# TensorE's usual expert path placed directly behind its test, and the keys of the last attention projected once and copied on the chip

## What is computed

```
def expert_block(args):
    xi, e = args
    hid = jax.nn.silu(xi @ w1[e]) * (xi @ w3[e])
    return hid @ w2[e]
```

```
h = rms_norm_2(x, norm_g) @ w_in
q, kv, gate_logits, z, qm, zm = split_cols_2(h, NSA_IN_SPLITS)
...
kc, vc, ks, vs, kw, vw = [t.reshape(b, s, g, hd).transpose(0, 2, 1, 3)
                          for t in jnp.split(kv, 6, axis=-1)]
...
k_cmp = compress_tokens(kc, pe_k, phik_w1, phik_w2)
v_cmp = compress_tokens(vc, pe_v, phiv_w1, phiv_w2)
```

## Time and profile before

| | us |
|---|---|
| median of 3 runs | 2123.06 |
| the profiled execution, its own time | 2122.02 |
| its span in the trace, first to last instruction | 2120.3 |
| TensorE busy | 1914.8 (90%) |
| VectorE busy | 669.2 |
| ScalarE busy | 338.5 |

### The profile page before, as it was taken

One profiled execution on the slowest core, in us unless ns is written; L12 is line 12 of the kernel. 1 busy time (PEld: TensorE's weight loads), 2 busy tenths in 40 slices (PEclk: granted clock), 3 DMA queues, 4 the chain that ended last, 5 costly groups with the idle time before them and its releaser, 6 DMA issues.

```text
span 2120.3 us, 27442 instructions
## 1 busy us (share of the span) xinstructions
PE 1914.8 (90%) x11750; PEld 1258.6 (59%) x11750; DVE 669.2 (32%) x1551; ACT 338.5 (16%) x738; POOL 81.0 (4%) x88
## 2 busy tenths in 40 slices
PE   5996669899999999898799999999979998999888
PEld 3745664566555555654466666566558875468754
DVE  2647543222221212671312122112142043301192
ACT  1112112100000000222310000000011123211161
POOL 0000200000000001000000000000100000000000
PEclk8997789999999999999799999999989999999899
DMA  9985505699999999663489999999974343095100
GB/s 353 377 263 192 159 2 238 277 427 427 427 428 428 427 427 414 242 253 124 170 335 423 421 427 428 424 426 426 424 274 159 119 164 109 1 223 170 57 1 30
DMA packets 158880, 588.20 MB, mean 277 GB/s; under 512 B 49612, under 2 KB 57424, under 8 KB 134096
## 3 DMA queue, kind: packets, MB, share of 16 engines
q1 hardware_dynamic: 127024, 560.59, 66.5%
q0 software_dynamic: 8256, 16.63, 2.5%
q10 hardware_dynamic: 23520, 9.86, 1.8%
HBM read 573.50 MB, written 25.23 MB: 282 GB/s over the span
## 4 chain that ended last, share of the span: by engine, by line
PE 68%; DMA 18%; DVE 8%; issue 2%; ACT 2%; PEld 1%; DVEq 1%; ACTq 0%; SPq 0%; PEldq 0%
DMA ring<-in_exp_w_dram 17%; PE bank L712 15%; PE bank L2069 14%; PE bank L2104 6%; PE bank L701 5%; PE bank L843 5%; PE bank L2037 3%; PE bank L2345 3%; PE bank L2335 2%; PE bank L2092 2%; DMA ring<-in_ada_w_dram 1%; PE bank L2045 1%; PE bank L419 1%; DVE pair_probs L3120 1%; DVE pair_probs L3135 1%
## 5 line engine op out<-in xcount | busy, mean ns | idle before, releaser
L2069 PE MATMUL bank<-ring,hidden_room 128*64 128x256 f32 x4096 | 462.2, 381 | 27.6 <-DMA ring<-in_exp_w_dram 24.5
L2069 PEld LDWEIGHTS bank<-ring,hidden_room 128*64 128x64 f32 x4096 | 318.6, 137 | 185.0 <-DMA ring<-in_exp_w_dram 42.1
L712 PE MATMUL bank<-hT,ring 128*128 128x256 f32 x1408 | 311.8, 384 | 5.0 <-ACTq L164 5.0
L712 PEld LDWEIGHTS bank<-hT,ring 128*128 128x128 f32 x1408 | 271.6, 193 | 43.8 <-issue 5.9
L2104 PE MATMUL bank<-ring,hidden_room 128*64 128x512 f32 x1024 | 233.9, 597 | 5.3 <-issue 1.8
L2244 DVE TENSOR_TENSOR hidden_room<-bank,hidden_room 128x256 f32<-128x256 f32 x64 | 27.2, 425 | 471.8 <-ACT hidden_room L2156 471.8
L2104 PEld LDWEIGHTS bank<-ring,hidden_room 128*64 128x64 f32 x1024 | 76.2, 136 | 121.2 <-issue 121.2
L2156 ACT ACTIVATE hidden_room<-bank 128x256 f32<-128x256 f32 x64 | 24.6, 384 | 744.1 <-PE bank L2069 744.1
L2037 PE MATMUL bank<-xn_kept,member 128*64 128x512 f32 x512 | 124.9, 607 | 17.1 <-issue 17.1
L701 PE MATMUL bank<-ring,hT 128*128 128x512 f32 (+2 forms) x288 | 116.0, 564 | 0.0
L1971 POOL DMA_INDIRECT expert_out<-hidden_room,route_spots x60 | 58.6, 977 | 1185.1 <-DVE hidden_room L2258 1171.7
(11 more groups left out here) (583 smaller groups left out, 1835.4 us busy)
## 6 DMA issues: line engine op xcount, KB each, us to landing
ring<-in_exp_w_dram SPq DMA_DIRECT2D x192, 2048.0 KB, 20.6
ring<-in_ada_w_dram SPq DMA_DIRECT2D x24, 2048.0 KB, 21.4
ring<-in_hawk_w_in_dram SPq DMA_DIRECT2D x15, 2048.0 KB, 9.0
ring<-in_even_w_in_dram SPq DMA_DIRECT2D x7, 2048.0 KB
ring<-in_gla_w_in_dram SPq DMA_DIRECT2D x6, 2048.0 KB, 23.3
ring<-in_nsa_w_in_dram SPq DMA_DIRECT2D x5, 2048.0 KB, 7.6
expert_out<-kc POOLq DMA_DIRECT2D x16, 512.0 KB, 12.6
ring<-in_even_w_out_dram SPq DMA_DIRECT2D x2, 2048.0 KB, 7.9
```

Source lines behind the costliest of these rows:

```text
L712: last = nc.tensor.matmul(pair[m // 2][0:rows, (m % 2) * T:(m % 2 + 1) * T], w[:, k, m * P:m * P + rows], src[:, k, :], start=(k == 0), st ...
L2069: last = nc.tensor.matmul(bank[2 + q][halves[half], part * FE // 2:(part + 1) * FE // 2], own[:, q, k % 4, k // 4, :], w[:, k, cols], star ...
```

## The change

Two things change. In `experts_stage`, TensorE's test is turned round (`<= CAP`), its usual path stands directly behind the test and the crowded path in the `Else`, both word for word as before. The tests of the other three engines stay as they are. In the sparse attention, one chunk of 512 columns (`kc` and `vc` in 256, `ks` in 128, `kw` in 128) takes the place of the two with doubled columns. ScalarE copies the halves that come out on the right partitions, and issues four transfers inside SBUF that bring the other halves (`to_halves`, `other_halves`); VectorE waits for these four ahead of the rows of the compression. The later entries of the plan, and ScalarE's work for them, move up by one.

```diff
-        cols_of(w, 0, KD, [(1024, 64)] * 2 + [(1088, 64)] * 2 + [(1152, 64)] * 2 + [(1216, 64)] * 2)
-        cols_of(w, 0, KD, [(1280, 64)] * 2 + [(1344, 64)] * 2 + [(1536, 64)] * 2 + [(1600, 64)] * 2)
+        cols_of(w, 0, KD, [(1024, 256), (1280, 128), (1536, 128)])
...
-                        with pe.If(fullest > CAP):
-
-                            pe.wait_ge(zeroed.sem, 1)
...
-                        with pe.Else():
+                        with pe.If(fullest <= CAP):
                             halves = [slice(0, CAP), slice(CAP, 2 * CAP)]
...
                             add_late(1)
+                        with pe.Else():
+
+                            pe.wait_ge(zeroed.sem, 1)
...
-                def to_pairs(pair):
-                    copies = []
-                    for b in range(2):
-                        src = pair[b][:, :].rearrange("p (m t) -> p m t", m=2)
-                        copies.append((pairT[0:HD, 2 * b:2 * b + 2, :], src[0:HD], 1.0))
-                        copies.append((pairT[HD:P, 2 * b:2 * b + 2, 0:T - 1], src[HD:P, :, 1:T], 1.0))
-                    return copies
+                def to_halves(pair):
+
+                    first_two, last_two = (pair[b][:, :].rearrange("p (m t) -> p m t", m=2) for b in range(2))
+                    return [(pairT[lower, 0::2, :], first_two[lower], 1.0), (plain[upper], first_two[upper], 1.0),
+                            (pairT[upper, 1::2, 0:T - 1], first_two[upper, :, 1:T], 1.0),
+                            (kT[lower, 0::2, :], last_two[lower], 1.0), (kT[upper, 1::2, :], last_two[upper], 1.0)]
+
+                def other_halves(act):
+
+                    act.wait_ge(evacuated_nsa.sem, evacuated_nsa.n)
+                    act.dma_start(pairT[upper, 0::2, 0:T - 1], pairT[lower, 0::2, 1:T]).then_inc(halves_in.up(16), 16)
+                    act.dma_start(pairT[lower, 1::2, :], plain[upper]).then_inc(halves_in.up(16), 16)
+                    act.dma_start(kT[upper, 0::2, :], kT[lower, 0::2, :]).then_inc(halves_in.up(16), 16)
+                    act.dma_start(kT[lower, 1::2, :], kT[upper, 1::2, :]).then_inc(halves_in.up(16), 16)
...
                     dve.wait_ge(evacuated.sem, evacuated.at(3))
+                    dve.wait_ge(halves_in.sem, halves_in.at(64))
...
-                                                ("channel", to_pairs), ("channel", to_channels(kT, 0)), ("token", to_tokens(vg, 0, 304)),
+                                                ("channel", to_halves), ("token", to_tokens(vg, 0, 304)),
                                                 ("channel", to_channels(zT, 0)), ("channel", to_channels(zT, 4)), ("channel", memory_query)], hT,
-                              scalar_work={0: load_operands, 4: sigmoids, 6: silu_of(zT[:, :, :]), 7: silu_of(mq[:, 2:4, :])},
+                              scalar_work={0: load_operands, 2: other_halves, 3: sigmoids, 5: silu_of(zT[:, :, :]), 6: silu_of(mq[:, 2:4, :])},
                               vector_work=rows_and_gates)
```

More of the change, by code:

```diff
@@ L2119, in _, with all_tokens @@
                             add_late(1)
+                        with pe.Else():
+                            pe.wait_ge(zeroed.sem, 1)
+                            for t in range(TT):
+                                for half in range(2):
+                                    nc.tensor.matmul(y[t][half][:, :], zero[:, 0:P], zero[:, :], start=True, stop=False)
+                            def all_tokens(pair, i):
+                                for q in range(2):
+                                    e = 2 * i + q
+                                    w1, w3, w2 = weights(pair, q)
+                                    for part in range(2):
+                                        weights_in(pe, pair, i, q, part)
+                                    for f in range(FT):
+                                        pe.wait_ge(hid_free.sem, hid_free.start + FT * e + f + 1)
+                                        for w, b in ((w1, f % 2), (w3, 2 + f % 2)):
+                                            for k in range(KD):
+                                                last = nc.tensor.matmul(bank[b][:, 0:T], w[:, k, f::FT], hT[:, k, :],
+                                                                        start=(k == 0), stop=(k == KD - 1))
+                                        last.then_inc(hid_ready.sem, 1)
+                                    weights_in(pe, pair, i, q, 2)
+                                    for f in range(FT):
+                                        pe.wait_ge(hid_free.sem, hid_free.start + 2 + FT * e + f + 1)
+                                        for t in range(TT):
+                                            for half in range(2):
+                                                last = nc.tensor.matmul(y[t][half][:, :], hid[:, f, t * P:(t + 1) * P],
+                                                                        w2[:, f, half * 512:(half + 1) * 512], start=False, stop=False,
+                                                                        skip_group_check=True)
+                                    last.then_inc(y_done.sem, 1)
+                            for a, b in spans(0, PAIRS):
+                                if a in after_pair:
+                                    memory_products(pe, a, bank[0], bank[1])
+                                    pe.wait_ge(memory_kept.sem, memory_kept.at(2 * bounds.index(a) + 2))
+                                with pe.Fori(a, b) as i:
+                                    all_tokens(a, i)
+                            for t in range(TT):
+                                for half in range(2):
+                                    last = nc.tensor.matmul(y[t][half][:, :], zero[:, 0:P], zero[:, :], start=False, stop=True)
+                            last.then_inc(summed.sem, 1)
+                            pe.wait_ge(sum_steps.sem, 2 * TT)
@@ L2926, in nsa_layer @@
                 mq = sb(st, "nsa_mem_q_gate", [P, 4, T])
[L2928 to L2934 removed]
+                lower, upper = slice(0, HD), slice(HD, P)
+                def to_halves(pair):
[9 more added lines that the diff above has]
+                    act.dma_start(kT[lower, 1::2, :], kT[upper, 1::2, :]).then_inc(halves_in.up(16), 16)
                 def memory_query(pair):
```

2 lines of the change are left out of this document (added).

## The result

| | us |
|---|---|
| the changed kernel, median of 13 runs | 2104.57 (2098.44 to 2118.11) |
| the kernel before beside it, median of 13 runs | 2125.40 (2119.26 to 2133.63) |
| ratio, with its 95% interval | 0.9904 [0.9886, 0.9922] |
| the changed kernel's profiled execution, and its span | 2098.69, 2097.0 |

It is faster by 1.0%, some 21 us, and the median lies 0.6 us from the forecast.

A forecast was written before the change was run, and what follows sets the result against it. The weights' stream was taken to bound the experts, mostly TensorE the rest. From 2122.0 us, -10.0 (tests), 0 (clock), +5.0 (end jumps) and -13.8 (chunk) gave 2103.2, predicted as a median of 2104, range 2097 to 2111.

The forecast's parts named there:

- The tests: TensorE's test ahead of the experts, both layers: usual path follows in sequence, so the branch stall goes; gain 10.0 us.
- The rival by which the stall belongs to the test itself: At the experts' test: the stall is not from distance, so the 10.0 us stay; 2114 us, chance 0.06.
- The clock: TensorE's clock level in layer 0's first pass and member products: taken as 0, from -2.0 to +2.2 us.
- The end jumps: End of the experts' usual path: TensorE's jump stalls 6.1 us, 2.5 beyond cover per layer; +5.0 us, 0 to +8.9.
- covered: Rival at the experts' ends: a stall of about 3.3 us fits the cover, no +5.0; 2099 us, chance 0.15.
- nearly all back: Rival at the experts' ends: two holes in a row or a fetch over 8 us, +8.9; 2108 us, chance 0.12.
- The chunk: Sparse attention's projection: one chunk of 32 TensorE products less, copies hidden; -13.8 us, from -13.8 to 0.
- The sum: Whole kernel: 2122.0 - 10.0 + 0 + 5.0 - 13.8 = 2103.2 us; with 1.0 for the median, 2104 predicted.

The follow-up runs named there:

- e_copies_late: The changed kernel with its four copies inside SBUF issued behind the projection's fifth chunk's eviction instead of the second's: 2114.43 us, ratio 0.9950 to the kernel before.
- e_nsa_only: The kernel before with the sparse attention's chunk change alone, TensorE's old order of paths kept: 2112.36 us, ratio 0.9934.

## Why the prediction was right

**The tests, -10.0: measured -10.0.** 2.80 in layer 0 (forecast 2.8) and 7.23 in layer 1 (7.2). The branch is 96 and 85 ns, below the 169 that I took. That the first product's gain reaches the end was right as well: the stream's restart moved by 7.25 us with it in layer 1, and in layer 0 the stretch from the first pass to the late sums stayed at 471.4 us (470.3 before, up to 473.7 where the first pass ran at the low clock). The rival by which the stall belongs to the test itself is refuted by the runs with and without code to jump over: the test is the same, the stall is where the far jump is.

**The clock, 0.** The level did change in a stretch that I had named: layer 0's first member products take 1.96 us in the changed kernel and 3.71 in the kernel before. Among the ten experiments they take 1.96 in three, 3.38 to 3.46 in six and 3.71 in the one with the old order; the first pass behind them takes 7.13 in five and 8.8 to 9.7 in five. That is inside -2.0 to +2.2, and most of it goes with the execution and not with the edit. I had not said that such draws lie in every stage: in the profiled pair they come to some 4.5 us (22.8 between the first record and the last, less 18.3).

**The end jumps, +5.0: measured +5.1.** 2.70 and 2.44 us, where I had 2.5 each. The stall is 6.2 and 6.0 us where I had taken 6.1, the middle between the 5.06 of layer 1's test and 7.2, which was the cheapest stall, 3.3, and the load that other small transfers feel. The experiment with quiet transfer engines bears out the reasoning: traffic is the difference, and an idle end gives 3.3 to 3.7. What the full stream adds is about 2.6 and not 3.9, so the upper bound was too high and hitting the middle so closely was in part luck. (The range's upper end is 4.4 a layer and 8.8 in all, not 4.45 and 8.9; nothing hangs on it.) Of the rivals, "covered" would have been true with no traffic, and "nearly all back" with a second hole, which did not come. The rule of the Trainium skill that I weighed ("Runtime: NRT & Kernel Launch", Instruction fetch mechanics: a taken branch to code that isn't held waits for a transfer) agrees with the packet of the instruction queue in every far jump, and with 5.9 to 6.2 us at the far target against 179 ns at the near one. By it the jump is paid once in either order, and so it is; what the change lives on is what stands beside it, 10.0 us uncovered at the tests and 5.1 at the ends.

**The chunk, -13.8: measured -13.44.** The stage has no gap, as forecast. The stretch is 109.7 and 110.0 us in the two traces with the old chunks and 95.6 to 96.6 in the nine with the new ones and the copies in their place, so the 0.4 that is missing is inside their scatter. The copies landed in 6 us, nearer to the 1.5 of the small transfer than to the 12.2 of the large one that bounded them; the rows began at 1926.5 and had 31 us to spare, which `e_copies_late` used up.

**The sum.** Own terms -18.3 us against the forecast's -18.8. That the median fell by 20.8 and the profiled execution by 23.3 is no more than the interval allows (16.6 to 24.2). The absolute number is right to 0.6 us because two small things cancel: the base was 2.3 us lower in the three runs shown than in the 13 of the result, and the difference is 1.8 us larger than forecast.

## What to carry to other kernels

Here a long path that is never run cost one code fetch wherever it was jumped over: put it so that the jump falls where the engine has nothing to do that others wait for, and give the engine's signal ahead of the jump, not behind it (2.8 us in the stretches here, 4.3 with VectorE's signal; no total resolves either). Look at the branch record and at what the transfer engines carry in that moment: the fetch took 3.3 to 3.7 us beside nothing and 5.9 to 6.2 under the weights' stream. Prices that are under a third of a percent of the kernel are to be read from stretches of the trace between two fixed events, not from the totals.

## What was not expected of the hardware

- The jump's price does not grow with the distance: 179 ns over eight products, 5.9 to 6.2 us over 80 products and over the whole path alike.
- The fetch takes 3.3 to 3.7 us although the transfer engines carried nothing but its one packet; under the stream it is 5.9 to 6.2 in all seven kernels that make the jump there.
- At the tests of the old order it went with the traffic too: 3.3 us at a share of 0.03 of the transfer engines, 4.3, 4.7 and 5.1 us at 0.45, 0.35 and 0.35. Among those three the order is not that of the share, and why stays open.
- The second hole of 3 us came in layer 1 of both kernels with the old order and never in layer 0. One packet of the instruction queue falls into it in both (between 1050.7 and 1053.6 us in the kernel before, 1053.8 and 1056.9 in `e_nsa_only`), so a second fetch fits, but it was not tried.
- A copy of 128 KB inside SBUF landed 5.9 to 6.2 us behind its issue in the changed kernel, beside a load of weights at full speed, and 7.3 to 8.5 us behind it in `e_copies_late`, also beside weights. How long it takes on idle engines no run shows.
